# The last pairs of a mixture-of-experts stage in another order

## Chip, core and metric

The kernel runs on one core of one Trainium2 chip. The metric is the device time of one execution in microseconds (us), as the median of several runs.

## The reference

Two transformer blocks on 256 tokens of width 1024, in float32. The first has a short convolution, a gated delta rule, a stick-breaking attention and a feed-forward part; the second has a differential and a neighbourhood attention and a mixture of experts. The change concerns the experts alone:

```python
logits = (hf @ w_router + b_router).astype(jnp.float32)
top_val, top_idx = lax.top_k(logits, TOP_K)          # 4 of 32 experts for each token
gates = jax.nn.softmax(top_val, axis=-1)
...
hh = xb @ w1[e] + b1[e]                              # 1024 -> 2048
return swiglu_clamped(hh) @ w2[e] + b2[e]            # 1024 -> 1024
...
out = jnp.einsum('tk,tkd->td', gates.astype(y.dtype), y)
```

Each token's result is the sum over its four experts, so the order in which experts are evaluated is free.

## The kernel before

After the two attention blocks the kernel evaluates 32 experts one after the other, at positions 0 to 31 of an order that it works out on the chip. The tokens of an expert are taken in passes of up to 32 (`CAP`). An expert with more than 32 tokens needs two or more passes, each with all the weights of the expert: it does all its up products first, one a pass (`up_pass`, matmul at line 1249, then the gather of the next pass's tokens at line 1224 and some transposes), and then its down products, one a pass (`down_pass`, the scatter of the pass before at line 1239, then the matmul at line 1266).

**The weights.** They are 12 MiB an expert, in six pieces of 2 MiB: four of w1 (piece 0 to 3) and two of w2 (4 and 5). They go through a ring of ten slots (`NSLOT`). SyncE issues all pieces in the order of use, from one queue (`expert_piece`, line 362). The first ten are loaded before the expert stage; every later piece n waits (`released`) until TensorE has used piece n - 10 in the last pass of its expert. For the pieces 0 to 3 of an expert that is its last up product, for the pieces 4 and 5 the middle and the end of its last down product. TensorE in its turn waits for the landing of each piece ahead of its first use (`loaded`).

**The order.** `_constants` lays out a table `rank`. On the chip each expert gets a key from its number of tokens, and its rank is the number of keys above it. Rank 0 and 1 are always experts 0 and 1, whose first pieces are loaded before the routing is known; ranks 2 to 31 go from the most tokens to the fewest. The last 32 entries of the table give for each position the rank that stands there: 0, 1, and then 15 pairs of a light and a heavy rank, (31 - i, 2 + i). The i are taken in triples. VectorE compares the table with the rank (lines 2332 and 2333) and gets the position, `POS`; a permutation matrix `PERM` (line 2335) then sorts first pass, number of passes and expert into the register table `passes`, which all engines read. In the order of before, the positions 2 to 7 hold the ranks 31, 2, 26, 7, 21, 12, and the positions 26 to 31 the ranks 27, 6, 22, 11, 17, 16.

**The expert loops.** TensorE has a written-out loop over 32 positions (line 1318 to 1331) with two inner loops over the passes; VectorE and ScalarE have the same as register loops (lines 2403 and 1812). SyncE loops over positions five at a time. Behind the last expert come the scatter of the last pass, a norm, the residual and the output (lines 1334 to 1337, 1835, 2424 to 2431).

Of the kernel before, what the change touches and what calls it, by code (L numbers as in the profile page):

```python
# [36 lines left out]
NE = 32  # L37
# [2397 lines left out]
def _constants():  # L2435

    c = np.zeros((P, NCONST), np.float32)
    i, j = np.arange(P)[:, None], np.arange(P)[None, :]

    def put(name, a):  # L2440
        o, w = CO[name]
        c[:, o:o + w] = a

    chunk = (i // GCH) == (j // GCH)
    put("ident", i == j)
    put("ones", 1.0)
    put("before", i < j)
    put("after", i > j)
    put("slot", j % CAP)
    put("count", np.broadcast_to(np.arange(NPMAX)[None], (P, NPMAX)))  # L2450
    put("upto", (i <= j) & chunk)
    put("same", chunk)
    row, col = np.arange(P)[:, None] % GCH, np.arange(GCH)[None, :]
    put("level", np.concatenate([-1.0 * (((row >> (l + 1)) == (col >> (l + 1))) & ((row >> l) % 2 == 0) & ((col >> l) % 2 == 1))
                                 for l in range(6)], 1))
    put("eye", row == col)
    put("later", BIG * (col < row))
    put("dist", np.concatenate([np.abs(np.arange(L)[None] - (P * t + i)) for t in range(T)], 1))
    col = np.arange(P)[:, None] % 64
    start = np.clip(col - 8, 0, 48)  # L2460
    cc = np.arange(64)[None]
    e = np.arange(NE)
    key = NE - 1 - e + 1.0e6 * (e == 0) + 0.5e6 * (e == 1)
    rank = np.zeros((P, 2 * NE + 8), np.float32)
    rank[:, 0:NE] = key
    rank[0:NE, NE], rank[0:NE, NE + 1] = key, e
    pairs = [(NE - 1 - i, 2 + i) for k in range(5) for i in (k, k + 5, k + 10)]
    rank[:, NE + 8:] = [0, 1] + [r for pair in pairs for r in pair]
    put("rank", rank)
    put("window", np.where((cc >= start) & (cc < start + 16), 0.0, -BIG))  # L2470
    return c


def _layout(inputs):
# [38 lines left out]
    def sl(a, n):  # L2513
# [22 lines left out]
    b1 = g["b1_2"][0].reshape(NE, 4, 256, 2).transpose(0, 1, 3, 2).reshape(NE, 2048)  # L2536
    return {
        "consts": _constants(), "vecs": vec, "stream": stream, "bada": bada.reshape(P, 1536),
        "rows": np.broadcast_to(rows, (P, 3072)), "natb": nb.transpose(2, 0, 1, 3).reshape(P, 4096),
        "w1": w1, "w2": w2, "b1": b1, "b2": g["b2_2"][0],  # L2540
# [17 lines left out]
```

## Time and profile before

| | |
|---|---|
| median of 3 runs | 1494.27 us (1492.65 to 1494.91) |
| profiled execution | 1494.06 us, span 1492.2 us |
| TensorE busy | 1330.6 us, 89% |
| VectorE, ScalarE busy | 536.0 us (36%), 468.6 us (31%) |
| moved by DMA | 509.69 MB, mean 342 GB/s |
| weights of experts | 192 pieces of 2 MiB |
| passes | 53 |

Times in the profile run from the start of the span. The rows of the page and of the trace stand further down, in numbered groups. In the chain of work ("chain") each row is a start, a duration, and what ran: an engine, the tile and the line, with the number of instructions. A matmul of float32 shows as two instructions, so one pass has 64 of line 1249 and 64 of line 1266. In the chain, an up product of a pass begins with a row "L1249 x8", because four matmuls for the bias (line 1254) stand behind the first eight.

### The profile page before, as it was taken

The page shows a single profiled execution, that of the slowest core. Times are in us where ns is not written, and L with a number is a line of the kernel's source. Part 1 is how long each engine was busy: PE and PEld are TensorE (multiplying, and loading weights), DVE is VectorE, ACT ScalarE, POOL GpSimd, SP SyncE. Part 2 cuts the span into 40 slices and gives each one's busy share as a digit, 9 for nine tenths or more (in the row PEclk, how much of TensorE's full clock was granted, in tenths as well). Part 3 has the DMA queues.
Part 4 walks back from the last instruction along what each step waited for, and adds up shares of the span by engine and source line. Part 5 has one row for each costly group of instructions (what it writes and reads, how often), then busy time and mean ns, then how long its engine had stood idle before and what let it go on. Part 6 is the DMA issues. An engine that isn't in the chain of part 4 may idle for free.

```text
span 1492.2 us, 32400 instructions
## 1 busy us (share of the span) xinstructions
PE 1330.6 (89%) x13170; PEld 789.9 (53%) x13170; DVE 536.0 (36%) x1088; ACT 468.6 (31%) x796; POOL 0.2 (0%) x4
## 2 busy tenths in 40 slices
PE   9999989999999989699998998869979799788995
PEld 8998669998689753234343433324424244233441
DVE  6842667875597751121121211111211121111112
ACT  6734434453446642122221221212212122112222
POOL 0000000000000000000000000000000000000000
PEclk9999999999999999899999999999989999999998
DMA  8332884455773499997999999999999999999995
GB/s 354 114 115 81 352 349 170 169 187 207 268 323 114 184 381 386 428 398 327 397 424 426 428 426 427 427 427 428 427 427 428 427 428 427 428 426 429 425 427 244
DMA packets 36421, 509.69 MB, mean 342 GB/s; under 512 B 4112, under 2 KB 4240, under 8 KB 5520
## 3 DMA queue, kind: packets, MB, share of 16 engines
q1 hardware_dynamic: 36336, 508.39, 82.1%
q8 instruction: 74, 1.21, 0.3%
q14 instruction: 11, 0.09, 0.0%
HBM read 507.33 MB, written 1.05 MB: 341 GB/s over the span
## 4 chain that ended last, share of the span: by engine, by line
PE 61%; DMA 25%; ACT 6%; DVE 5%; issue 3%; SPq 0%; DVEq 0%; ACTq 0%
PE acc L1249 19%; DMA low<-in_w 17%; PE acc L1266 11%; PE acc L488 8%; DMA low<-in_stream 6%; PE acc L1239 4%; PE acc L1224 3%; DMA high_part<-in_w 2%; PE acc L526 2%; ACT w_hi L1404 2%; PE acc L943 1%; PE acc L1231 1%; PE acc L981 1%; PE acc L527 1%; ACT high_part L1820 1%
## 5 line engine op out<-in xcount | busy, mean ns | idle before, releaser
L1249 PE MATMUL acc<-low,high_part 128*32 128x512 f32 x2720 | 338.9, 631 | 61.6 <-DMA low<-in_w 50.6
L1249 PEld LDWEIGHTS acc<-low,high_part 128*32 128x32 f32 x2720 | 95.9, 113 | 259.9 <-issue 182.1
L2389 DVE TENSOR_SCALAR high_part<-acc 128x256 f32<-128x256 f32 x53 | 22.5, 425 | 548.0 <-PE acc L1249 548.0
L1266 PE MATMUL acc<-low,high_part 128*32 128x256 f32 x2752 | 157.8, 381 | 2.3 <-DMA low<-in_w 2.3
L1410 DVE TENSOR_TENSOR w_lo<-low,w_hi 128x4096 fp32r<-128x4096 f32 x30 | 132.6, 4424 | 46.1 <-ACT w_hi L1404 45.7
L1818 ACT ACTIVATE high_part<-high_part 128x256 f32<-128x256 f32 x53 | 22.1, 416 | 394.0 <-DVE high_part L2389 394.0
L1404 ACT ACTIVATE w_hi<-low 128x4096 fp32r<-128x4096 f32 x28 | 101.4, 3630 | 70.3 <-DMA low<-in_stream 68.2
L1266 PEld LDWEIGHTS acc<-low,high_part 128*32 128x32 f32 x2752 | 84.8, 110 | 68.9 <-issue 14.3
L1249 PE MATMUL acc<-high_part 128*32 128x512 f32 x672 | 84.2, 624 | 20.3 <-DMA high_part<-in_w 17.8
L488 PE MATMUL acc<-x_hi,w_hi 128*128 128x256 f32 x352 | 87.9, 289 | 6.1 <-DVE low L2013 5.4
L1239 PE MATMUL acc<-high_part 32*128 32x256 f32 x864 | 77.1, 425 | 14.2 <-ACT high_part L1831 11.1
L488 PE MATMUL acc<-x_lo,w_hi 128*128 128x256 f32 x352 | 87.3, 288 | 0.0
L1818 ACT ACT_TABLE_LOAD x53 | 68.0, 1283 | 44.4 <-issue 44.0
L1831 ACT ACTIVATE high_part<-acc 128x256 f32<-128x256 f32 x53 | 20.4, 384 | 170.1 <-PE acc L1266 170.1
L488 PEld LDWEIGHTS acc<-x_hi,w_hi 128*128 128x128 f32 x352 | 69.4, 197 | 7.1 <-DVE low L2013 5.6
L2416 DVE COPY high_part<-high_part 128x256 f32 x53 | 15.6, 294 | 150.8 <-PE acc L1239 150.8
L488 PEld LDWEIGHTS acc<-x_lo,w_hi 128*128 128x128 f32 x352 | 69.4, 197 | 0.0
L1224 PE MATMUL acc<-high_part 128*32 128x256 f32 x864 | 62.1, 404 | 0.4 <-DVE high_part L2352 0.4
L1249 PEld LDWEIGHTS acc<-high_part 128*32 128x32 f32 x672 | 23.7, 111 | 67.1 <-issue 43.2
L1224 PEld LDWEIGHTS acc<-high_part 128*32 128x32 f32 x864 | 34.0, 119 | 45.1 <-issue 38.3
L1239 PEld LDWEIGHTS acc<-high_part 32*128 32x128 f32 x864 | 34.6, 183 | 40.7 <-ACT high_part L1831 21.7
L1231 PE MATMUL acc<-high_part 128*128 128x128 f32 x108 | 23.9, 303 | 27.4 <-ACT high_part L1820 26.4
(495 smaller groups left out, 1836.2 us busy)
## 6 DMA issues: line engine op xcount, KB each, us to landing
low<-in_w SPq DMA_DIRECT2D x154, 2048.0 KB, 27.3
low<-in_stream SPq DMA_DIRECT2D x46, 2048.0 KB, 8.4
high_part<-in_w SPq DMA_DIRECT2D x38, 2048.0 KB, 27.6
high_part<-in_natb SPq DMA_DIRECT2D x1, 2048.0 KB, 19.0
high_part<-in_rows SPq DMA_DIRECT2D x1, 1536.0 KB, 13.0
high_part<-in_x SPq DMA_DIRECT2D x2, 512.0 KB, 4.5
out<-high_part SPq DMA_DIRECT2D x2, 512.0 KB, 2.7
high_part<-in_consts SPq DMA_DIRECT2D x1, 868.0 KB, 12.0
```

The lines of the kernel that those rows point to most:

```text
L488: return nc.tensor.matmul(o, w[:, k, cols], x[:, k, :], **flags)
L526: return nc.tensor.matmul(o, w[:, k, cols], x[:, k, :], skip_group_check=True, **flags)
L1224: last = mm(flat[32 * q:32 * q + 32, 3072:3328], SEL[:, t, :], H2R[:, t, 256 * q:256 * q + 256], start=(t == 0), stop=(t == T - 1))
L1231: last = nc.tensor.transpose(flat[:, 3584 + 128 * b:3584 + 128 * b + 128], GS[:, 128 * b:128 * b + 128], ident)
L1239: last = mm(flat[:, o:o + 256], SGT[r, 128 * t:128 * t + 128], YS[r, :], start=False, stop=False, skip_group_check=True)
L1249: last = mm(flat[32 * q:32 * q + 32, 2048:2560], XG[:, b, 32 * kk:32 * kk + 32], wp[:, 2048 * b + 512 * q:2048 * b + 512 * q + 512], start ...
L1266: last = mm(flat[32 * q:32 * q + 32, 2816:3072], AT[:, 128 * (c % 2) + 32 * (c // 2):128 * (c % 2) + 32 * (c // 2) + 32], wp[:, 1024 * (c ...
L1404: eng.activation(HI[i % 2], slot, ACT.Copy).then_inc(S("hi_act"), 1)
L1410: v.tensor_tensor(LO[s], ring[:, s, :], HI[i % 2].bitcast(F32), ALU.subtract).then_inc(S("lo_ready"), 1)
L1818: f(SIG, GLU, ACT.Sigmoid, scale=1.702).then_inc(S("sig"), 1)
L1831: f(YS, flat[:, 2816:3072], ACT.Copy).then_inc(S("y_in"), 1)
L2389: ts(GLU, flat[:, 2048:2304], 7.0, None, ALU.min).then_inc(S("glu"), 1)
```

## The change

In every triple of pairs the second and the third pair change place. For k = 0 to 4 the triple was i = k, k + 5, k + 10; it is now k, k + 10, k + 5. The rest of the table and all the code stay.

```diff
@@ -2464,7 +2464,7 @@
     rank = np.zeros((P, 2 * NE + 8), np.float32)
     rank[:, 0:NE] = key
     rank[0:NE, NE], rank[0:NE, NE + 1] = key, e
-    pairs = [(NE - 1 - i, 2 + i) for k in range(5) for i in (k, k + 5, k + 10)]
+    pairs = [(NE - 1 - i, 2 + i) for k in range(5) for i in (k, k + 10, k + 5)]
     rank[:, NE + 8:] = [0, 1] + [r for pair in pairs for r in pair]
     put("rank", rank)
```

The positions 2 to 7 now hold the ranks 31, 2, 21, 12, 26, 7, and the positions 26 to 31 the ranks 27, 6, 17, 16, 22, 11.

## Rows read from the trace of the kernel before

**Rows 1.** The page: busy engines, GB/s of 40 slices, passes of VectorE

```profile
PE 1330.6 (89%) x13170; PEld 789.9 (53%) x13170; DVE 536.0 (36%) x1088; ACT 468.6 (31%) x796; POOL 0.2 (0%) x4
GB/s 354 114 115 81 352 349 170 169 187 207 268 323 114 184 381 386 428 398 327 397 424 426 428 426 427 427 427 428 427 427 428 427 428 427 428 426 429 425 427 244
L2389 DVE TENSOR_SCALAR high_part<-acc 128x256 f32<-128x256 f32 x53 | 22.5, 425 | 548.0 <-PE acc L1249 548.0
```

**Rows 2.** Stretches: length, busy of engines, TensorE clock, DMA share, GB/s

```profile
648.00:668.00 20.00, 18.26 (x216) 8.21 (x211) 4.93 (x16) 5.17 (x11) 0.00 (x0) 1.00 0.92 372
668.00:698.00 30.00, 28.03 (x394) 13.69 (x394) 5.77 (x21) 5.53 (x12) 0.00 (x0) 1.00 0.73 301
698.00:742.00 44.00, 40.29 (x466) 16.39 (x458) 8.22 (x28) 10.44 (x20) 0.00 (x0) 1.00 1.01 426
742.00:760.00 18.00, 17.04 (x222) 7.98 (x222) 3.67 (x14) 3.99 (x8) 0.00 (x0) 1.00 0.89 360
760.00:1478.00 718.00, 616.77 (x6958) 256.30 (x6950) 121.53 (x408) 147.63 (x287) 0.00 (x0) 0.96 1.00 425
```

**Rows 3.** Waits of SyncE: us in total, times, longest

```profile
SPq L362 <- PE acc L1249: 415.0, 122, 44.3
SPq L362 <- PE acc L1266: 324.7, 60, 22.9
```

**Rows 4.** Chain, 684 to 762 us, positions 4 to 7

```profile
684.10 1.07 PE acc L1249 x8
...
699.42 1.06 PE acc L1249 x8
...
719.18 1.06 PE acc L1249 x8
...
746.13 1.07 PE acc L1249 x8
...
761.41 1.07 PE acc L1249 x8
```

**Rows 5.** Chain at positions 9 and 10; issues at 744 and 857 us

```profile
792.02 24.87 DMA low<-in_w
...
859.43 1.06 PE acc L1249 x8
...
low<-in_w SPq DMA_DIRECT2D x2, 2048.0 KB, 9.9
...
857.53 2.06 SPq L362 DMA_DIRECT2D high_part<-in_w  x2
...
high_part<-in_w SPq DMA_DIRECT2D x1, 2048.0 KB, 13.2
```

**Rows 6.** Chain, 1407 to 1481 us, positions 29 to 31

```profile
1407.98 1.06 PE acc L1249 x8
...
1417.64 1.07 PE acc L1249 x8
...
1438.77 1.07 PE acc L1249 x8
...
1442.83 35.91 DMA low<-in_w
...
1478.78 1.98 PE acc L1266 x32
```

**Rows 7.** Chain at position 27: landed data, then the second up product

```profile
1350.10 3.56 PE acc L1249 x16
...
1356.01 1.06 PE acc L1249 x8
```

**Rows 8.** Instructions in order of time, position 31, last w1 piece

```profile
1469.06 3.06 PE L1249 MATMUL acc<-high_part 128*32 128x512 f32 x16 [2.98 <-DMA high_part<-in_w]
```

**Rows 9.** Stretches around position 27, columns as in rows 2

```profile
1350.00:1354.00 4.00, 3.90 (x28) 1.19 (x32) 0.29 (x1) 0.00 (x0) 0.00 (x0) 0.57 1.00 426
1354.00:1374.00 20.00, 18.55 (x188) 6.87 (x180) 4.79 (x17) 6.19 (x12) 0.00 (x0) 1.00 1.01 430
```

## Prediction

> **What bounds the kernel now.** I read the page first, then the expert stage by stretches, then what the DMA issuing queue waits for, then the chain of work around the experts that change place. The page shows two resources near full: TensorE is busy for 89% of the span, and the transfers run at 424 to 429 GB/s in nearly every slice of the second half [rows 1]. The reader has to find out which of them sets the end of the expert stage. The stretches settle it: from 760 to 1478 us the DMA share is 1.00 at 425 GB/s, while TensorE is busy in 617 of 718 us [rows 2]. The chain says the same at the end: 35.91 us of it is one transfer, and the last half of the down product (1.98 us) starts 0.05 us after that transfer lands [rows 6]. So the end is the landing of the last weight piece plus a short tail. A piece is 2 MiB, which at 427 GB/s is 4.91 us; an expert (six pieces) is 29.5 us, whatever its number of passes.
>
> Since the transfers alone set the end, they can lose time only where a piece can't be issued because its slot isn't free. SyncE does wait on the slots, for 415 and 325 us in total on TensorE's two products [rows 3], but this costs only where the ten slots run empty of requests. Three stretches show it: 648 to 668 us at 372 GB/s, 668 to 698 at 301, 742 to 760 at 360 [rows 2]. Against 427 GB/s they lose 2.6, 8.8 and 2.8 us, 14.2 together.
>
> **Who causes which loss.** Positions count from 0. The chain gives the passes of an expert by its up products: one at 684.10 (position 4), then one expert that begins at 699.42, has its third up product at 719.18 and hands over to position 6 at 746.13, then position 7 at 761.41 [rows 4]. The page has 53 passes in all [rows 1]. The routing of the reference, evaluated on its inputs, gives the same passes by position: 1,1,1,4,1,3,1,2,1,3,1,2,1,2,1,3,1,2,1,2,1,3,1,2,1,2,1,3,1,2,1,1. Rank 7 has 68 tokens (3 passes), rank 12 has 36 (2), rank 11 has 37 (2), rank 16 has 28 (1); ranks 26, 21, 22 and 17 have 1 each. The six pieces of a position free the slots of the pieces ten later, so the four passes of position 3 hold back the last pieces of position 4 and the third of position 5: these are the losses up to 698 us. The three passes of position 5 hold back the third piece of position 7, which is issued at 744 us: the loss at 742 to 760.
>
> **What the change does, part by part.** The table of ranks has the same number of entries; the planner's instructions, every loop body, the 53 passes and the 192 pieces stay, so all of that costs nothing. In each triple of pairs the second and third change place. For the triples k=1, 2, 3 the exchanged pairs are both 1+2 passes, so nothing moves in time. Two exchanges are left.
>
> (a) Positions 5 and 7: 3 and 2 passes become 2 and 3. A one-pass expert takes 15.3 us (684.10 to 699.42), a three-pass one 46.7 (699.42 to 746.13) [rows 4], a two-pass one 30.8 (1407.98 to 1438.77) [rows 6]. So position 5 ends 15.9 us earlier and its last down pass frees the slot for the third piece of position 7 at about 728 instead of 744 us. That piece's turn at the transfers is about 747, so the loss of 2.8 us goes. The losses to 698 us stay, because position 3 is where it was. What is late next: position 7 now has three passes. Position 6 starts at 730.2, position 7 at 745.5, and there it meets its data. The fourth piece of position 9 lands at 792.02 + 24.87 = 816.9 [rows 5]; twelve pieces earlier that is 758.0, and 755.2 with the loss gone. From the landing of the fourth piece to the next up product is 5.9 us (1350.10 to 1356.01) [rows 7], so position 7 has its second up product at 761.1, its third 9.7 later, and hands over 26.9 after that (719.18 to 746.13 [rows 4]), at 797.7; position 9 begins at 813.0, position 10 (46.7 later) at 859.7, where it was 859.4 before [rows 5]. The first piece that hangs on this is the third of position 11, issued at 857.5 with 13.2 us to its landing; the one issued into an empty queue at 744 took about 8 (the pair has a median of 9.9, the second of it issued 1.7 us after the first and landing 5 to 6 after) [rows 5]. Its slack is thus about 5 us before; after, its turn comes 2.8 us earlier and its issue 0.3 later, so some 2 us are left. Further on TensorE waits for its data again (position 13 and later), and everything moves with the transfers. Result of (a): the last landing 2.8 us earlier. Bounds: 0, if the slack isn't there, and 3.5, if the small dent of 698 to 742 (426 GB/s) goes too. I take 2.8, the row of the very stretch.
>
> (b) Positions 29 and 31: 2 and 1 passes become 1 and 2. No slot is held longer, and no transfer is lost at the end. But the last expert now has a second up pass and a second down pass behind the last data. Before: the last piece lands at 1478.73, the down product ends at 1480.76 [rows 6]: 2.0 us of work behind the transfers. After, with T the last landing: the fourth piece lands two pieces before it, at T - 9.8 (in the trace 1469.06 to 1478.78 [rows 6, 8]). The second up product starts 5.9 us later [rows 7], at T - 3.9. From the second up product of a two-pass expert to the start of the next expert the trace has 1438.77 - 1417.64 = 21.1 us, of which 0.4 is the step to the next expert [rows 6], so the last down product ends at T + 16.8. The two last w2 pieces land during the second up pass and hold nothing up. Cost of (b): 16.8 - 2.0 = +14.8 us. Its cover is only the 9.8 us in which the w2 pieces land; without that it would be some 25. Behind the last down product everything is as it was (1480.76 to 1492.2). Bounds: 13.5, if the first up product's end is as little delayed as at full clock (the 3.06 us of the last quarter [rows 8] against 1.9 unimpeded), and 16.5, if one stretch at the lower clock falls into the second pass.
>
> **Sum.** Profiled execution: 1494.06 us with a span of 1492.2. -2.8 + 14.8 = +12.0: span 1504.2, time 1506.1. The median of the runs of before is 1494.27, 0.2 above the profiled one, so against it the change is +0.8%.
>
> **Rivals.** (1) *The exchange frees all the dry time.* If the transfers were late at 648 to 698 us through position 5 as well, all 14.2 us would go: 1494.06 - 14.2 + 14.8 = 1494.7, no change. For it: the largest loss is right ahead of position 5. Against it: transfers are already at 301 GB/s from 668 us, when position 5 hasn't begun (699.42 [rows 4]); only position 3's last down pass is running. 2%.
> (2) *Nothing gained in the middle.* The slack of 2 us at position 11 is used up or position 7's third pass dries the queue elsewhere: 1494.06 + 14.8 = 1508.9. It decides as soon as an issue into a near-empty queue takes over 10 us to land; the rows have about 8 and 13.2 [rows 5]. 6%.
> (3) *Faster.* The last expert's extra pass costs nothing, so only (a) is left: 1494.06 - 2.8 = 1491.3. The place is position 31, and the point is 32 tokens: if rank 11 had at most 32, it would have one pass. The trace has two up products at position 29 (1407.98 and 1417.64), which is rank 11 in the order of before [rows 6], and the routing has 37. 2%.
> (4) *The last expert runs at the lower clock.* In an expert that waits for data the granted clock falls: 0.57 in 1350 to 1354 us, between full and the 1.2 GHz level, after waits for the pieces; but it is 1.00 in the 20 us behind, in the second and third up pass and the start of the down passes [rows 9]. If the second up pass (7.3 us) and both down passes (3.7 each) ran at 1.2 GHz, their products would take twice as long: up to 14.7 us more, 1520.8; one short stretch would be 1.7 us, 1507.8. The Trainium skill ("TensorE: Matmul & The Clock Gate", section "HAM oscillation — how this bites in real kernels") says that TensorE that waits for data drops to the low clock and begins the next work at it. By that rule the positions 29 to 31, which now all wait for data, would each begin slow; the trace agrees for the first pass and contradicts it for the following ones. 4% for over 3 us.
>
> **How the numbers follow.** The forecast, +10 to +15 us, has 86%; rival 2 lies at its upper end. Low end of the range: 1506.1 - 1.3 (lower bound of b) - 0.7 (upper bound of a) and 1 us for the spread of runs (1492.65 to 1494.91): 1503.1. High end: 1508.9 and 0.7 of the clock: 1509.6. The range 1503.1 to 1509.6 leaves out rivals 1 and 3, most of 4, and some error of terms. A measurement of this kernel can tell 0.2%, 3 us, from no change. Faster 2%, same 3% (rival 1 and mishaps), slower 95%.
>
> **What would show it.** Steps: the stretch 742 to 760 us at about 427 GB/s, with 648 to 698 as before; two up products at position 5 and three at position 7; the last landing at about 1475.9; a second up product at about 1472 and two down products behind the last landing, the last ending at about 1492.8, 16.8 us behind it. The prediction is wrong if the last landing moves by more than 4 us, if a new stretch under 420 GB/s appears between 760 and 900 us, or if the work behind the last landing is well off 17 us up to the end of the down products.

## Result and the profile after

The change made the kernel slower, about as forecast: 1505.8 us (median of 6 runs, 1504.96 to 1507.42) against 1494.3 (6 runs, 1491.65 to 1495.08). The ratio is 1.0082 with a 95% interval of 1.0069 to 1.0095, which is 12.3 us more (10.3 to 14.2); the forecast was 1506.1, 12.0 more.

The profiled execution of after has a span of 1505.6 us, 13.4 more than before. Not all of this is the change. Below, the chain of work of after around positions 4 to 7 (start, us, what ran).

```profile
685.37 1.07 PE acc L1249 x8
...
700.69 1.07 PE acc L1249 x8
...
710.64 1.07 PE acc L1249 x8
...
731.59 24.67 DMA low<-in_w
756.31 1.92 PE acc L1249 x16
...
760.61 1.07 PE acc L1249 x8
...
770.26 1.06 PE acc L1249 x8
...
797.25 1.06 PE acc L1249 x8
```

Position 4 begins at 685.37, where it was 684.10 [rows 4]. Up to there both kernels do the same work with the same experts, so these 1.3 us are a difference between executions. I measure everything from this point: from the start of position 4 to the end of the span it is 808.1 us before and 820.2 after, a difference of 12.1. The chain also shows the exchange: position 5 now has two up products (700.69 and 710.64), and position 7 has three (its first begins at 747.1 with data that had been there, then waits 0.45 us for the third piece and 2.96 for the fourth, which lands at 756.26; 760.61 and 770.26 are the second and third).

The stretches of after (length, busy PE, PEld, DVE, ACT, POOL, TensorE clock, DMA share, GB/s):

```profile
648.00:668.00 20.00, 18.32 (x214) 7.95 (x206) 4.67 (x15) 5.16 (x11) 0.00 (x0) 1.00 0.92 375
668.00:698.00 30.00, 28.00 (x380) 13.68 (x384) 5.65 (x19) 5.52 (x12) 0.00 (x0) 1.00 0.73 300
698.00:742.00 44.00, 40.56 (x480) 17.20 (x472) 8.02 (x27) 10.43 (x20) 0.00 (x0) 1.00 1.01 428
742.00:760.00 18.00, 13.73 (x164) 5.33 (x160) 2.91 (x10) 2.84 (x5) 0.00 (x0) 1.00 1.01 429
760.00:1475.00 715.00, 605.31 (x6823) 251.96 (x6826) 119.42 (x403) 145.97 (x283) 0.00 (x0) 0.96 1.00 425
```

Against [rows 2], 742 to 760 us went from 360 to 429 GB/s, while the two stretches in which the four-pass expert of position 3 holds the slots stayed at 375 and 300 (372 and 301 before). No new dry stretch (a time in which the transfers have too few requests) appeared: 760 to 1475 us has 425 GB/s, as 760 to 1478 had before.

The chain at the end of after:

```profile
1421.38 45.93 DMA high_part<-in_w
1467.31 0.04 issue
1467.35 2.97 PE acc L1249 x16
...
1473.24 1.06 PE acc L1249 x8
...
1484.68 3.63 PE acc L1266 x64
...
1490.50 3.63 PE acc L1266 x64
```

The transfer that ends the chain is no longer the last piece but the fourth of position 31, landing at 1467.31. The chain doesn't show the last landing. Two more pieces of 4.9 us each put it at about 1477.1, and in before the same two took 9.7 us (1469.02 to 1478.73); all landings called "about" below are worked out like this. No transfer is in the chain behind 1467.31: it is a second up product from 1473.24 and two down products, the last ending at 1494.13, with short steps of ScalarE between them. From 1477 on the transfers are idle:

```profile
1477.00:1494.00 17.00, 15.82 (x220) 7.39 (x212) 3.49 (x11) 2.70 (x7) 0.00 (x0) 1.00 0.01 1
```

### The profile page after: what moved, and what is told of

Read it like the earlier page. It is cut to its first block, busy times and chain, and to the rows that moved or that the text cites. A ratio compares the mean times of both kernels' runs of the same rounds, so it can differ in the third digit from the quotient of the medians.

```text
span 1505.6 us, 32400 instructions
## 1 busy us (share of the span) xinstructions
PE 1331.7 (88%) x13170; PEld 791.0 (53%) x13170; DVE 536.2 (36%) x1088; ACT 468.3 (31%) x796; POOL 0.2 (0%) x4
## 4 chain that ended last, share of the span: by engine, by line
PE 61%; DMA 25%; ACT 6%; DVE 4%; issue 3%; SPq 0%; DVEq 0%; ACTq 0%
PE acc L1249 18%; DMA low<-in_w 14%; PE acc L1266 11%; PE acc L488 8%; DMA low<-in_stream 6%; DMA high_part<-in_w 5%; PE acc L1239 4%; PE acc L1224 3%; PE acc L526 2%; ACT w_hi L1404 2%; PE acc L943 1%; PE acc L1231 1%; PE acc L981 1%; PE acc L527 1%; ACT high_part L1820 1%
## 5 line engine op out<-in xcount | busy, mean ns | idle before, releaser
L1249 PE MATMUL acc<-low,high_part 128*32 128x512 f32 x2688 | 334.4, 629 | 75.9 <-DMA low<-in_w 65.4
L1266 PE MATMUL acc<-low,high_part 128*32 128x256 f32 x2816 | 163.4, 384 | 3.3 <-DMA low<-in_w 3.3
L2416 DVE COPY high_part<-high_part 128x256 f32 x53 | 15.5, 293 | 150.9 <-PE acc L1239 150.9
```

What stands on the lines that cost most here:

```text
L1249: last = mm(flat[32 * q:32 * q + 32, 2048:2560], XG[:, b, 32 * kk:32 * kk + 32], wp[:, 2048 * b + 512 * q:2048 * b + 512 * q + 512], start ...
L1266: last = mm(flat[32 * q:32 * q + 32, 2816:3072], AT[:, 128 * (c % 2) + 32 * (c // 2):128 * (c % 2) + 32 * (c // 2) + 32], wp[:, 1024 * (c ...
```

## The experiments

My theory: the landing of the last weight piece sets the end, a dry stretch that costs 2.8 us goes, and the second pass at the last position costs 14.8 us behind the last data. The rivals: the gain in the middle is absent or larger, the cost at the end comes from TensorE being late or slow in general, or the placing of particular experts matters. All experiments change only the table of ranks and leave no part of the computation out. Times within one group share the runs of the kernel before (median 1492.9 us for the first four, 1493.8 for the last two), so ratios are compared.

### The first triple alone

```diff
-    pairs = [(NE - 1 - i, 2 + i) for k in range(5) for i in (k, k + 5, k + 10)]
+    pairs = [(NE - 1 - i, 2 + i) for k in range(5) for i in ((k, k + 10, k + 5) if k == 0 else (k, k + 5, k + 10))]
```

> Only the first triple is exchanged (positions 5 and 7 have 2 and 3 passes), the end is as before. Theory (the transfers set the end; a dry stretch of 2.8 us goes): 1494.3 - 2.8 = 1491.5 us, the last landing 2.8 us earlier, 742 to 760 us at 427 GB/s, 648 to 698 us unchanged. Rival that the slack at position 11 is used up: 1494.3. Rival that the dry time ahead of position 5 goes as well: about 1480.

Measured: 1490.84 us (11 runs), ratio 0.9987 (0.9978 to 0.9996), which is 1.9 us less (0.6 to 3.3). Stretches and the end of the chain of this kernel, whose position 4 begins at 681.60, 2.5 us earlier than before, so that the stretches are taken 4 us earlier:

```profile
664.00:694.00 30.00, 27.78 (x376) 13.54 (x380) 5.65 (x19) 5.71 (x13) 0.00 (x0) 1.00 0.74 303
694.00:738.00 44.00, 40.56 (x482) 17.34 (x476) 8.03 (x27) 10.37 (x20) 0.00 (x0) 1.00 1.01 428
738.00:756.00 18.00, 13.94 (x168) 5.31 (x160) 2.90 (x10) 2.90 (x6) 0.00 (x0) 1.00 1.00 426
```

```profile
1436.39 36.57 DMA low<-in_w
1473.00 1.98 PE acc L1266 x32
```

The dry stretch ahead of position 7 is gone, the one ahead of position 5 (303 GB/s) is not, and no other took its place. From the start of position 4 to the last landing it is 1472.96 - 681.60 = 791.4 us, against 1478.73 - 684.10 = 794.6 before: 3.3 less. The work behind the last landing is 2.0 us, as before. So the gain is real and of the size forecast; "nothing gained" and "all dry time gained" both fall. This kernel beats the change by far, and the kernel before by 0.13%, an interval that leaves out 1 by little.

### The last triple alone

The same line with `k == 4` in place of `k == 0`.

> Only the last triple is exchanged (positions 29 and 31 have 1 and 2 passes). Theory (one up and one down pass more behind the last data): 1494.3 + 14.8 = 1509.1 us, with the last landing where it is before and the last down product ending 17 us behind it. If part of the slowdown of the change came from the first triple, this one would be slower by less than 14 us.

Measured: 1508.91 us (4 runs), ratio 1.0104 (1.0088 to 1.0119), 15.5 us more (13.1 to 17.8). Chain at the end:

```profile
1423.38 44.88 DMA high_part<-in_w
1468.30 3.43 PE acc L1249 x16
...
1474.11 1.07 PE acc L1249 x8
...
1491.26 3.63 PE acc L1266 x64
```

The fourth piece lands at 1468.26, the last thus at about 1478.1, and the last down product ends at 1494.89: 16.8 us behind it. The stretch 742 to 760 us is dry as before (362 GB/s). The two parts together explain the change: 0.9987 times 1.0104 is 1.0091, inside the interval of the change (1.0069 to 1.0095).

### The change with its last pair turned

```diff
-    pairs = [(NE - 1 - i, 2 + i) for k in range(5) for i in (k, k + 5, k + 10)]
+    pairs = [(NE - 1 - i, 2 + i) for k in range(5) for i in (k, k + 10, k + 5)]
+    pairs[-1] = pairs[-1][::-1]
```

> The change with its last pair turned, so that the two-pass expert stands at position 30 and a one-pass expert at 31. Theory (only passes behind the last data cost): 1491.5 to 1492.5 us; the last down product ends 2 to 3 us behind the last landing. Rival (TensorE is behind because the two passes come late at all, or because the last positions wait more and run at the lower clock): 1500 or more.

Measured: 1489.57 us (8 runs), ratio 0.9981 (0.9967 to 0.9994), which is 2.8 us less (0.9 to 4.9); the expected times are 1.8 to 2.8 us below the kernel before. One position earlier, the two passes cost almost nothing. Chain at the end:

```profile
1401.41 32.32 DMA low<-in_w
1433.77 3.64 PE acc L1249 x16
...
1440.59 1.06 PE acc L1249 x8
...
1461.72 1.06 PE acc L1249 x8
...
1473.06 3.64 PE acc L1266 x64
```

The fourth piece of position 30 lands at 1433.73; eight pieces later, at about 1473.0, is the last landing. Position 31 begins right behind position 30, its down product starts at 1473.06 without a wait and ends at 1476.70, 3.7 us behind the last landing. I had expected 2 to 3. So position 30's second pass leaves TensorE late by some 1.7 us, a small remainder that the profile shows and the timing can't: by ratio this kernel isn't told apart from the first experiment, while its stretch from position 4 to the end is 2.0 us longer. That TensorE is "late in general", or slow after waits, falls: only passes behind the last data cost much.

### The middle triples alone

The same line as in the first experiment with the condition `0 < k < 4`.

> Only the three middle triples are exchanged, whose exchanged pairs have one and two passes each. Theory: no difference, 1494.3 within 1.5 us. Rival (which expert and which weights stand where matters, by the tokens or by where the weights lie in memory): over 3 us either way.

Measured: 1493.80 us (10 runs), ratio 1.0004 (0.9994 to 1.0015). Which of two experts with equal passes stands where makes no difference that can be measured.

### The expert of four passes later

```diff
-    rank[:, NE + 8:] = [0, 1] + [r for pair in pairs for r in pair]
+    order = [0, 1] + [r for pair in pairs for r in pair]
+    order[3], order[15] = order[15], order[3]
+    rank[:, NE + 8:] = order
```

with `pairs` as in the first experiment.

> The first triple exchanged, and the expert of four passes at position 15 instead of 3, a three-pass one at position 3. Theory (four passes hold the slots so long that the queue runs dry by 8 to 9 us wherever they stand, and three don't): the dry stretch of 668 to 698 us is gone and stands behind position 15 (about 1040 to 1080 us) instead; the sum of the losses is unchanged, 1491.5 us. Rival (the dry time is one of the start of the stage, where the ring isn't yet filled, or of heavy experts close together): it goes, and the time is 1480 to 1485.

Measured: 1492.50 us (10 runs), ratio 0.9987 (0.9976 to 0.9998), the same ratio as the first experiment's. Stretches (the third takes in the two behind it):

```profile
648.00:668.00 20.00, 18.42 (x258) 9.19 (x254) 4.38 (x14) 3.47 (x9) 0.00 (x0) 1.00 1.01 428
668.00:698.00 30.00, 27.71 (x326) 11.77 (x318) 5.45 (x19) 8.11 (x14) 0.00 (x0) 1.00 1.01 427
1000.00:1050.00 50.00, 46.17 (x572) 21.07 (x572) 9.09 (x32) 11.30 (x23) 0.00 (x0) 1.00 0.77 316
1026.00:1044.00 18.00, 16.16 (x250) 8.41 (x246) 3.06 (x11) 2.56 (x7) 0.00 (x0) 1.00 0.56 224
1044.00:1050.00 6.00, 5.91 (x60) 2.31 (x64) 0.00 (x0) 1.40 (x2) 0.00 (x0) 1.00 0.95 396
```

The dry stretch has moved with the expert: 648 to 698 us is at 427 and 428 GB/s, and a dry stretch stands at 1000 to 1050 us. It is deepest at 1026 to 1044, during the expert's down products, which loses (427 - 224) / 427 x 18 = 8.6 us, but it begins during its up products, and the whole loses (427 - 316) / 427 x 50 = 13.0 us. The whole at position 3 is 11.4 us in before (2.6 and 8.8 in the prediction's working). The expectation had it at 1040 to 1080 us, behind position 15; it stands within position 15. So this loss belongs to the four passes that hold the ten slots, at both positions tried, not to the start of the stage nor to the heavy expert that follows. This is also why the exchange of positions 5 and 7 couldn't free it. Whether it is somewhat dearer at position 15 isn't settled: from the landing of the first piece of position 3 to the last landing it is 864.7 us here and 864.0 in the first experiment (867.8 before), and the ratios of the two are the same.

### Three passes at the last position

The change, with `order[27]` and `order[31]` exchanged in the same manner.

> The change with a three-pass expert at position 31 and the two-pass one at 27: the suspected cost doubled. Theory (each further pass at the last position costs a whole up period of 9.7 and a down period of 5.8 us, since the cover of the landing w2 pieces is used up by the second pass): 15.5 us more than the change, about 1521.4 us, and 32.5 us from the last landing to the end of the last down product. Rival (half-clock passes behind the waits): over 1525. Rival (the end isn't set by the passes of the last expert): 1506.

Measured: 1520.94 us (4 runs), ratio 1.0178 (1.0158 to 1.0198). The change has 1.0082, so the third pass adds 0.0096, which is 14.3 us of 1494, with some 3.5 us of uncertainty since both ratios have their intervals; by the traces it is 15.1 (27.2 less 12.1 in the table below), where 15.5 were expected. Its chain at the end:

```profile
1416.53 46.91 DMA high_part<-in_w
1463.48 2.82 PE acc L1249 x16
...
1469.37 1.06 PE acc L1249 x8
...
1479.04 1.07 PE acc L1249 x8
...
1490.37 3.63 PE acc L1266 x64
...
1496.19 3.63 PE acc L1266 x64
...
1502.02 3.63 PE acc L1266 x64
```

The up products are 9.7 us apart, the down products 5.8, as the working behind [rows 4] had them. The last ends at 1505.65; the last landing is at about 1463.44 + 9.8 = 1473.2, so 32.4 us of work stand behind it, where 32.5 were expected. The granted clock is lower just behind the wait and full in the tail:

```profile
1463.00:1466.00 3.00, 2.52 (x16) 0.70 (x20) 0.00 (x0) 0.00 (x0) 0.00 (x0) 0.73 0.78 333
...
1479.00:1506.00 27.00, 24.98 (x334) 11.98 (x334) 4.40 (x15) 5.47 (x12) 0.00 (x0) 1.00 0.00 0
```

### All kernels on one scale

Single profiled executions, each from the start of position 4 to the end of the span (for the experiment with the four passes moved, this start isn't comparable). The start differs by up to 4 us between executions. Most of it arises ahead of position 3; from the first up product of position 3 to the start of position 4 it is 73.1 us in before and 71.1 in the last triple alone, with the same work.

| kernel | position 4 starts | span | difference | against before |
|---|---|---|---|---|
| before | 684.10 | 1492.2 | 808.1 | |
| after | 685.37 | 1505.6 | 820.2 | +12.1 |
| first triple alone | 681.60 | 1486.5 | 804.9 | -3.2 |
| last triple alone | 683.26 | 1506.4 | 823.1 | +15.0 |
| last pair turned | 681.31 | 1488.2 | 806.9 | -1.2 |
| middle triples alone | 683.80 | 1492.1 | 808.3 | +0.2 |
| three passes last | 681.85 | 1517.1 | 835.3 | +27.2 |

## Why the prediction was right, point by point

**What bounds the kernel.** The prediction said that the last landing sets the end and that TensorE's 86% hides below it. Moving passes between the middle positions (middle triples, four passes later) changed nothing but where the transfers run dry, and passes behind the last landing cost their full length. Both fit transfers that set the end.

**Part (a), -2.8 us.** After has -3.0 by the landings (the fourth piece of position 31 lands at 1467.31, where its product began at 1469.06 [rows 8]: 1.7 earlier, and 1.3 more for the start), the first experiment -3.2 by its span from position 4 and -1.9 (-3.3 to -0.6) by timing. One step of its working was off without harm. I took 5.9 us from the landing of the fourth piece of position 7 to its second up product, from position 27 [rows 7]. It was 760.61 - 756.26 = 4.35: the clock hadn't fallen there, and the last 16 matmuls took 1.92 us instead of 3.56. Position 10 began at 858.92, less 1.27 for the start 857.65, where I had 859.7. The slack at position 11 was therefore about 4 us, not 2; the rival that it is used up was weaker than I made it. The upper bound of 3.5 us doesn't follow from its reason either: 698 to 742 us at 426 GB/s instead of 427 loses 0.1 us, so the working gives 2.9. That would put the low end of the range at 1503.7 instead of 1503.1, and the result lies well inside both.

**Part (b), +14.8 us.** Here the 5.9 us held (1467.31 to 1473.24), and from there to the end of the down products it is 20.9 us (20.7 assumed). The work behind the last landing is about 17.0 us in after and 16.8 in the last triple alone, against 16.8 forecast and 2.0 before. The last triple alone costs +15.0 by its trace and +15.5 (13.1 to 17.8) by timing. Less the 1.3 us of the later start, after has its last landing at about 1475.8, its second up product at 1472.0 and the end of the last down product at 1492.9; the prediction had 1475.9, 1472 and 1492.8. So the sum of +12.0 is right because both parts are, not because two errors cancel.

**What costs nothing.** The middle triples: 1.0004 (0.9994 to 1.0015).

**The rivals.** That all dry time goes fell with the stretch at 300 GB/s; the experiment with four passes later shows why. That the last expert has one pass fell with the second up product at 1473.24. The clock: a last expert that waits for its data does run slow while it waits. The last quarter of its first up product took 2.97 us in after, 3.43 in the last triple alone and 2.82 with three passes, against 1.92 at full clock. This is in the 5.9 us already. Then it is granted in full, 1.00 over the 17 us behind 1477, and the second and third passes keep their 9.7 and 5.8 us. The first up product of position 31 in after, in order of time, with the waits in brackets:

```profile
1452.76 1.06 PE L1249 MATMUL acc<-low,high_part 128*32 128x512 f32 x8 [3.06 <-DMA low<-in_w]
...
1453.84 1.07 PE L1249 MATMUL acc<-low,high_part 128*32 128x512 f32 x8
1457.56 3.41 PE L1249 MATMUL acc<-low,high_part 128*32 128x512 f32 x16 [2.65 <-DMA low<-in_w]
1462.45 1.92 PE L1249 MATMUL acc<-high_part 128*32 128x512 f32 x16 [1.48 <-DMA high_part<-in_w]
1467.35 2.97 PE L1249 MATMUL acc<-high_part 128*32 128x512 f32 x16 [2.98 <-DMA high_part<-in_w]
```

The Trainium skill ("TensorE: Matmul & The Clock Gate", section "HAM oscillation — how this bites in real kernels") tells of a matmul kernel in which every tile behind a wait for data starts at the low clock. The trace agrees in part: all four quarters follow a wait, and two of them are slow (3.41 and 2.97 us) while two run at full clock (1.06 and 1.07 us for half a quarter each, and 1.92). The cost here is 1 to 1.5 us for the last expert, in its last quarter, not a slow tail. The prediction's remark that positions 29 to 31 would now all wait for data is wrong for position 29: it starts at 1406.25, right behind position 28, and TensorE's first wait for a piece comes with position 30, 2.2 us ahead of 1423.40.

**Not settled.** Why single executions reach position 4 up to 4 us apart wasn't looked into; it lies ahead of everything the change touches. That TensorE's lateness in the experiment with the last pair turned costs 1.7 us rests on one profile and on a last landing that was worked out. Why the stream of weights ends at half its rate (below) is open too.

## What to carry to other kernels

In a stage that streams weights at the full rate of the transfers, as in this one, extra passes over resident weights are free in the middle as long as the slots don't run dry, and cost nearly their full length at the last position: put the shortest work last, and look at how much of it stands behind the last landing. When an order is changed to remove one dry stretch, check every place that the rule touches; here a rule for five triples gained 3 us in the first, nothing in three and lost 15 us in the last, and restricting it to the first triple beats both kernels (ratio 0.9987), as does the change with its last pair turned (0.9981, not told apart from it). Which expert causes a dry stretch is found by asking which last pass frees the slot of the piece that is issued late.

## What the runs showed that I had not expected

The four-pass expert has its dry time at position 3 and at position 15 alike, 11.4 and 13.0 us by the rates. I had thought it possible that the fuller queue of the later position would cover some of it. Ten slots of 4.9 us are 49 us of transfers, and an expert of four passes holds TensorE some 62 us (four times 15.5, the difference of a two-pass and a one-pass expert); the difference of 13 us is of the same size, but how the slots come free step by step wasn't worked out.

The stream of weights doesn't end at its full rate, in any of these kernels. In before it moves 428 GB/s up to 1470 us and then 178 over 1471 to 1478, until the last landing at 1478.73; in after it is 194 over 1469 to 1476, in the first triple alone 211 over 1464 to 1472, and the DMA share is 0.42 to 0.50 in these stretches. The last landings are 4.9 us apart all the same. The prediction said that no transfer is lost at the end, and none is lost by the change, since before and after have the same tail; but the mean of 425 GB/s for 760 to 1478 us hides some 4 us ((427 - 178) / 427 x 7) that neither order touches.

And a wait for data doesn't always lower the granted clock: position 7 of after waited 2.96 us for its fourth piece and ran its next 16 matmuls in 1.92 us; position 31 waited 2.98 us for its fourth and took 2.97.
